# First expert stage of a fused transformer block: half of its first 64 tiles multiply both activation parts at once, in 512 columns, and VectorE adds the halves

## What is computed

```
q  = (xc @ w_q).reshape(t, PEER_HEADS, 2, PEER_QDIM // 2)
sc = einsum('thpc,hpnc->thpn', q, sub_keys)
v_half, i_half = lax.top_k(sc, 16)            # per half key
cand = v_half[:, :, 0, :, None] + v_half[:, :, 1, None, :]
top_s, pos = lax.top_k(cand.reshape(t, heads, -1), 16)
g = softmax(top_s)                             # weights of the 16 picks
act = gelu(einsum('thkd,td->thk', u_tab[expert], xc))
w = g * act
out = einsum('thk,thkd->td', w, v_tab[expert])
```

## Time and profile before

| | us |
|---|---|
| median of three runs | 2315.11 (2314.62 to 2317.86) |
| the profiled execution, its own time | 2312.29 |
| its span in the trace | 2310.5 |
| TensorE busy | 2226.4 (96%) |
| VectorE busy | 1700.3 (74%) |
| ScalarE busy | 1169.5 (51%) |
| mean granted clock of TensorE | 0.986 |

### The profile page before, as it was taken

How to read it: one execution, slowest core, us unless ns; L and a number is a source line. 1 busy time by engine, 2 the same in 40 slices (tenths; PEclk the granted TensorE clock), 3 DMA queues, 4 the chain that set the end, 5 groups by cost and what they waited for, 6 DMA issues and landing times.

```text
span 2310.5 us, 44458 instructions
## 1 busy us (share of the span) xinstructions
PE 2226.4 (96%) x15960; PEld 2011.1 (87%) x15960; DVE 1700.3 (74%) x3205; ACT 1169.5 (51%) x1688; POOL 0.2 (0%) x4
## 2 busy tenths in 40 slices
PE   7999899899999999999999998999999999999998
PEld 7998787689999999878888887899999998888886
DVE  5787676855998687798755567569977778986554
ACT  5566344545555555444444455545564554444444
POOL 0000000000000000000000000000000000000000
PEclk9999999799999999999999999999999999999999
DMA  6444244234545444455555542435554444555553
GB/s 262 178 180 152 92 149 149 73 107 149 177 169 190 156 168 168 146 172 173 183 190 190 191 153 79 155 137 173 181 179 158 172 165 149 178 166 190 190 190 137
DMA packets 95589, 376.37 MB, mean 163 GB/s; under 512 B 10861, under 2 KB 10989, under 8 KB 92817
## 3 DMA queue, kind: packets, MB, share of 16 engines
q1 hardware_dynamic: 95504, 375.29, 47.0%
HBM read 374.20 MB, written 1.05 MB: 162 GB/s over the span
## 4 chain that ended last, share of the span: by engine, by line
PE 70%; DVE 16%; ACT 2%; issue 2%; DMA 0%; ACTq 0%; SPq 0%; DVEq 0%
PE bank L328 21%; PE bank L330 21%; PE bank L329 21%; DVE tile_lo L2269 4%; PE bank L2003 3%; DVE e_hidden L2295 2%; DVE e_hidden L2289 2%; DVE e_hidden L2301 1%; DVE e_hidden L2341 1%; DVE e_hidden L2343 1%; DVE e_hidden L2339 1%; PE bank L2087 1%; DVE tile_lo L260 0%; PE bank L295 0%; PE bank L875 0%
## 5 line engine op out<-in xcount | busy, mean ns | idle before, releaser
L329 PE MATMUL bank<-a_lo,tile_hi 128*128 128x256 f32 x2688 | 756.1, 281 | 0.0
L328 PE MATMUL bank<-a_hi,tile_hi 128*128 128x256 f32 x2176 | 623.1, 286 | 16.4 <-DVE tile_lo L2269 5.3
L330 PE MATMUL bank<-a_hi,tile_lo 128*128 128x256 f32 x2176 | 613.7, 282 | 0.0
L329 PEld LDWEIGHTS bank<-a_lo,tile_hi 128*128 128x128 f32 x2688 | 511.4, 190 | 0.0
L2221 ACT ACTIVATE tile_hi<-wbuf 128x1024 fp32r<-128x1024 f32 x248 | 263.4, 1062 | 388.3 <-PE bank L330 385.4
L328 PEld LDWEIGHTS bank<-a_hi,tile_hi 128*128 128x128 f32 x2176 | 413.1, 190 | 24.1 <-issue 13.7
L2393 DVE TENSOR_TENSOR tile_lo<-wbuf,tile_hi 128x1024 fp32r<-128x1024 f32 x256 | 312.3, 1220 | 164.2 <-ACT tile_hi L2221 164.2
L330 PEld LDWEIGHTS bank<-a_hi,tile_lo 128*128 128x128 f32 x2176 | 413.3, 190 | 0.0
L328 PE MATMUL bank<-tile_hi,hidden_hi 128*128 128x512 f32 x1024 | 407.4, 398 | 5.0 <-DVE hidden_lo L2396 5.0
L330 PE MATMUL bank<-tile_hi,hidden_lo 128*128 128x512 f32 x1024 | 402.7, 393 | 0.0
L329 PE MATMUL bank<-tile_lo,hidden_hi 128*128 128x512 f32 x1024 | 402.4, 393 | 0.0
(11 more groups left out here) (355 smaller groups left out, 3112.6 us busy)
## 6 DMA issues: line engine op xcount, KB each, us to landing
wbuf<-in_peer_u SPq DMA_DIRECT2D x256, 512.0 KB, 3.5
wbuf<-in_peer_v SPq DMA_DIRECT2D x256, 512.0 KB, 3.5
wbuf<-in_w_in SPq DMA_DIRECT2D x16, 2048.0 KB, 7.7
wbuf<-in_peer_q SPq DMA_DIRECT2D x32, 512.0 KB, 4.0
wbuf<-in_hyb_in SPq DMA_DIRECT2D x16, 512.0 KB, 3.6
wbuf<-in_mla_uq SPq DMA_DIRECT2D x9, 512.0 KB, 3.5
wbuf<-in_mla_in SPq DMA_DIRECT2D x8, 528.0 KB, 3.3
wbuf<-in_w_v SPq DMA_DIRECT2D x2, 2048.0 KB, 7.2
```

Of the source, the lines that this page charges most:

```text
L328: nc.tensor.matmul(out, hi[:, cols], other_hi, start=start, stop=False, **kw)
L329: nc.tensor.matmul(out, hi[:, cols], other_lo, start=False, stop=False, **kw)
L330: return nc.tensor.matmul(out, lo[:, cols], other_hi, start=False, stop=stop, **kw)
```

## The change

In both expert layers, for tiles 0 to 63 (`SPLIT` = 8 rounds), every second pair of tiles (the pairs that begin at a tile number divisible by four) is multiplied in another way. For each step `k` there are two matmuls instead of three: the weight low part by the activation high part, 256 columns, into the right half of a bank; and the weight high part by both activation parts at once, 512 columns, into the whole bank. So the left half collects high by low and the right half the other two. Each tile of such a pair has a bank of its own, 2 and 3. The other pairs keep the three products and all use bank 1.

The two halves have to be added. ScalarE copies the left halves of both banks into `hidden` (128x512), VectorE adds the right halves to them in place (128x512), and ScalarE puts the sum through Gelu in place. TensorE may begin the next such pair once VectorE has added the one before (`parts_added`). VectorE's add of the pair `a - 1, a` stands in its list behind the low part of tile `a + 4`. The semaphores of the first layer that are now cleared for reuse add eight clears to SyncE's list behind the loads of the first U.

```
+def paired_products(nc, out, main, hi, lo, parts, other_hi, k, start, stop):
+    cols = slice(k * P, (k + 1) * P)
+    nc.tensor.matmul(out[:, main * S:(main + 1) * S], lo[:, cols], other_hi, start=start, stop=False, skip_group_check=True)
+    return nc.tensor.matmul(out, hi[:, cols], parts, start=False, stop=stop, skip_group_check=True)
...
+        def split_experts(r, j):
+            q, slot = j // 2, (M_U + j) % SLOTS
+            pe.wait_ge(lo_done, STEP * r + j + M_U + 1)
+            if j % 4 == 0:
+                pe.wait_ge(parts_added, 2 * r + q // 2 + 1)
+            if j % 4 == 2:
+                pe.wait_ge(bank_free, 2 * r + q // 2 + 2)
+            for k in range(KT):
+                if q % 2 == 0:
+                    last = paired_products(nc, bank[:, 2 + j % 2, :], 1, tile_hi[:, slot, :], tile_lo[:, slot, :],
+                                           g["a_parts"][:, :, k, :], h_hi[:, k, :], k, k == 0, k == KT - 1)
+                else:
+                    last = three_products(nc, bank[:, 1, (j % 2) * S:(j % 2 + 1) * S], tile_hi[:, slot, :], tile_lo[:, slot, :],
+                                          h_hi[:, k, :], h_lo[:, k, :], k, k == 0, k == KT - 1)
...
-        with pe.Fori(0, FIRST_WEIGHING) as r:
+        with pe.Fori(0, SPLIT) as r:
             for j in range(STEP):
-                experts(r, j)
+                split_experts(r, j)
+        pe.wait_ge(parts_added, 1 + ADDED)
+        for j in range(STEP):
+            experts(SPLIT, j)
...
+        def split_tile(r, j):
+            q = j // 2
+            if j % 4 == 1:
+                act.wait_ge(used, STEP * r + 2 * q + M_U + 2)
+                nc.scalar.activation(pair(r, q), split_banks(slice(0, S)), ACT.Copy).then_inc(low_kept, 1)
+            elif j % 4 == 3:
+                act.wait_ge(parts_added, 2 * r + q // 2 + 2)
+                gelu(r, q)
+            else:
+                act.wait_ge(used, STEP * r + j + M_U + 1)
+            rounded_u(r, j)
+            if j % 4 == 3:
+                nc.scalar.activation(pair(r, q - 1), pair(r, q - 1), ACT.Gelu).then_inc(added_done, 1)
...
+        def add_parts(a):
+            if a % SLOTS == 1 and a < SPLIT * STEP:
+                part = hidden[:, a - 1:a + 1, :]
+                dve.wait_ge(low_kept, a // SLOTS + 1)
+                nc.vector.tensor_tensor(part, split_banks(slice(S, 2 * S)), part, ALU.add).then_inc(parts_added, 1)
+
         def next_rest():
             nonlocal tiles
             if tiles < (FIRST_WEIGHING - 1) * STEP:
                 rest(tiles, tiles % SLOTS)
+                add_parts(tiles - SLOTS)
                 tiles += 1
```

More of the change, by code:

```diff
@@ L131, in build @@
         _, h_at = fixed("h_T", [P, KT, S])
-        _, other_at = fixed("h_other", [P, KT, S])
+        fixed("h_other", [P, KT, S])
         wbuf, wbuf_at = fixed("wbuf", [P, NW, SLOTS * TILE])
@@ L159, in build @@
             "tile_lo": rounded("tile_lo", [P, SLOTS, TILE], wbuf_at + 2 * BUF),
-            "a_hi": rounded("a_hi", [P, KT, S], other_at),
-            "a_lo": rounded("a_lo", [P, KT, S], h_at),
+            "a_parts": rounded("a_parts", [P, 2, KT, S], h_at),
             "hidden_hi": rounded("hidden_hi", [P, SLOTS, S], x_at),
@@ L170, in build @@
         }
+        g["a_lo"], g["a_hi"] = (g["a_parts"][:, part, :, :] for part in range(2))
         early = []
@@ L408, in first_layer @@
         conv_step, pool_step, conv_sig, gate_sig, z_sig, gated, v_done, v_kept = (
-            sem(n) for n in ("conv_step", "pool_step", "conv_sig", "gate_sig", "z_sig", "gated", "v_done", "v_kept"))
+            g["early_sem"](n) for n in ("conv_step", "pool_step", "conv_sig", "gate_sig", "z_sig", "gated", "v_done", "v_kept"))
         sig_flat = sig[:, :, :].rearrange("p a t -> p (a t)")
@@ L1932, in expert_layer @@
     sc_kept = [sem(f"{tag}_sc_kept{n}") for n in range(2)]
-    bank_free = sem(f"{tag}_bank_free")
+    bank_free, low_kept, parts_added, added_done = (sem(f"{tag}_{n}") for n in ("bank_free", "low_kept", "parts_added", "added_done"))
     half_step, best_step, pick_step, soft_step, exps_done, picks_turned, picks_kept = (
@@ L2022, in expert_layer, with split_banks @@
     FIRST_WEIGHING = ROUNDS - WEIGHING
+    SPLIT = FIRST_WEIGHING - 1
+    ADDED, OTHERS = 2 * SPLIT, 2 + 2 * SPLIT
+    def split_banks(cols):
+        return bank[:, 2:4, cols]
     at = 0
@@ L2099, in experts @@
             if j % 2 == 0:
-                pe.wait_ge(bank_free, STEP // 2 * r + j // 2 + 1)
+                pe.wait_ge(bank_free, STEP // 2 * r + j // 2 + OTHERS - 1 - STEP // 2 * SPLIT)
             for k in range(KT):
@@ L2103, in experts @@
                                       h_hi[:, k, :], h_lo[:, k, :], k, k == 0, k == KT - 1)
+            last.then_inc(used, 1)
+        def split_experts(r, j):
[12 more added lines that the diff above has]
+                                          h_hi[:, k, :], h_lo[:, k, :], k, k == 0, k == KT - 1)
             last.then_inc(used, 1)
@@ L2177, in scalar @@
         act.sem_inc(bank_free, 2)
+        act.sem_inc(parts_added, 1)
         def rounded_u(r, j):
@@ L2196, in tile, with pair @@
             rounded_u(r, j)
+        def pair(r, q):
+            return hidden[:, bass.ds(STEP * r + 2 * q, 2), :]
+        def split_tile(r, j):
[11 more added lines that the diff above has]
+                nc.scalar.activation(pair(r, q - 1), pair(r, q - 1), ACT.Gelu).then_inc(added_done, 1)
         def rounds(first, end):
@@ L2201, in rounds @@
                     tile(r, j)
-        rounds(0, FIRST_WEIGHING - 1)
+        with act.Fori(0, SPLIT) as r:
+            for j in range(STEP):
+                split_tile(r, j)
         act.wait_ge(soft_step, NT)
@@ L2350, in vector @@
             rest(a, a % SLOTS)
+            add_parts(a - SLOTS)
         for t in range(NT):
@@ L2371, in vector @@
         dve.wait_ge(picks_kept, 5)
-        dve.wait_ge(bank_free, 2 + HALF // 2)
+        dve.wait_ge(bank_free, OTHERS + HALF // 2 - 2 * ADDED)
+        dve.wait_ge(added_done, ADDED)
         one_hots(dve, 0, 0, 0, first_done[0], hots_done[0])
```

## The result

| | before | changed |
|---|---|---|
| median, us | 2314.86 (2310.33 to 2317.86, 4 runs) | 2334.62 (2333.33 to 2337.53, 4 runs) |
| ratio | | 1.0097, 95% interval 1.0084 to 1.0110 |
| profiled execution, its span | 2312.29, 2310.5 | 2337.53, 2335.7 |
| first stage, layer 1 and layer 2 | 211.67, 211.69 | 224.64, 223.29 |

The changed kernel is slower by 0.97%. The predicted time was 2336.1 us, in a range from 2330 to 2342.

The account below looks back on a forecast made before the run. VectorE's list was taken to bound tiles 5 to 57, TensorE's the rest. Each layer: 11.2 - 0.51 - 0.16 = 10.5 us; both layers 21.0, so 2315.1 + 21.0 = 2336.1 us, range 2330 to 2342.

Parts of the forecast that it names:

- The bound: First stage: VectorE's list sets the time for tiles 5 to 57 (3.05 us a tile against 2.86), TensorE's behind them.
- The adds: VectorE's list: 16 adds of 128x512 a layer, 0.60 us each, 13 of them ahead of tile 57's low part.
- The table load: ScalarE's 1.28 us load moves to the second pair, removing VectorE's idle time at tile 5: 0.6 us gained.
- The new wait: TensorE's tile 56 needs the add of pair 52, 53, behind tile 57's low part; it starts at 741.1, 11.2 us later.
- The wide matmuls: TensorE's paired tiles: a step goes from 0.357 to 0.352 us, saving 0.04 us a tile, 0.16 for four.
- The sum without the clock: First stage, each layer: 11.2 us later at tile 56, less 0.51 and 0.16, gives 10.5 us.
- the handover: At tile 56: TensorE waits for one more tile of VectorE's list plus the add before the path becomes TensorE's.
- The step that failed: TensorE's 3.6 us waits ahead of tiles 28 and 56: halved clock given chance 0.12, total 2339 to 2343 us.
- The rival: Half clock behind tile 56's wait loses 1.5 to 3 us a layer; tile 28's loss is taken up; chance 0.12.
- What was to show it: Profile signs: VectorE without gaps, one TensorE wait per four tiles up to 3.6 us, tile 56 near 741, clock 1.00.

Follow-up runs that it names:

- 24 spare matmuls: Changed kernel plus 24 extra 256-column matmuls ahead of TensorE's waits at tiles 28 and 56 in each layer: 2337.45 us, ratio 1.0099.
- the respaced one: Changed kernel with a low part after every 5 cells instead of 8 in the two selections over 128 values: 2325.44 us, ratio 1.0050.

## Why the prediction was right, and where it was off

**The number.** 2336.1 us against 2334.62 is closer than the account behind it. In the profiled execution the stages grew by 24.6 us and the span by 25.2, where 21.0 was forecast; that the median grew by only 19.8 is scatter between runs, and part of the closeness is luck, since a second set of runs of the same kernel stands 24.4 over the kernel before. The parts below are therefore judged by the stages.

**The bound.** Right. VectorE's list bounds tiles 5 to 57: sixteen adds alone, thirteen of them ahead of the low part of tile 57, bring 7.8 us a layer, taking them away brings back all of it, and spreading the same selection over six tiles more takes 5.6 us off the kernel before.

**The adds.** 0.60 us a step was taken from the earlier trace rows, and 0.60 was measured (742.00 to 742.60). The Trainium skill's rule, by which the next operation waits until the pipeline is empty ("VectorE: DVE Perf Modes", Terms), would have made it 0.68, taken as the end of the record; the trace doesn't agree.

**The table load.** The 0.54 us of idle time ahead of the low part of tile 5 are gone: it starts at 574.65, 8.25 us behind tile 0, and before it was 573.56 - 564.60 = 8.96. That is 0.71, and 0.6 was taken.

**The new wait.** The low part of tile 57 was to begin at 739.2 and tile 56 at 741.1, on the clock on which tile 0 begins at 564.60. Tile 0 is at 566.40 now, 1.80 later, so the rows above give 739.05 and 740.94.

**The wide matmuls.** 0.04 us a tile was taken. From tile 56 to the transposes, without a fall (24 spare matmuls), it is 786.77 - 741.10 = 45.67 us; before it was 776.27 - 729.90 = 46.37, less the 0.51 of the wait for tile 57, 45.86. So four paired tiles save 0.19, and 0.16 was expected.

**The sum without the clock.** 10.5 us a layer predicted, 222.00 - 211.67 = 10.3 measured. Its parts: the run without adds gives back 0.9 (210.80; 0.6 + 0.16 in the prediction), the adds in the list bring 7.8 on top of that, 218.6, and the handover is what is left up to 222.0, 3.4 us (in the prediction 11.2 - 7.2 - 0.51 = 3.5). That the three simply add up is taken here, not shown by a run of its own; the run with the adds sooner, 2.85 less where 2.8 was expected, bears the handover out.

**The step that failed.** The chance of 0.12 for a fall of the clock. I knew two rows, 2.16 us of idle time without a fall and one idle time with a fall, which is 5.05 us long in the trace, and put 3.6 us between them with little weight on the fall, though it lies midway. And the trace of the kernel before held two more falls, which the prediction doesn't use: one behind 2.50 us and one behind 1.69 us of idle time. Three rows of its timeline, two of them with the window behind them (the granted clock is the third number from the end):

```profile
349.86 1.97 PE L295 MATMUL bank<-cst,x_tok 128*128 128x128 f32 x8 [5.05 <-DVE x_tok L1044]
...
960.48 0.50 PE L328 MATMUL bank<-tile_hi,hidden_hi 128*128 128x512 f32 x1 [2.50 <-DVE hidden_lo L2396]
962.00:965.00 3.00, 3.00 (x16) 2.09 (x15) 3.00 (x7) 0.14 (x1) 0.00 (x0) 0.50 0.47 175
...
1337.62 0.63 PE L328 MATMUL bank<-tile_hi,a_hi 128*128 128x352 f32 x1 [1.69 <-DVE a_lo L308]
1337.00:1340.00 3.00, 2.38 (x8) 2.41 (x9) 0.76 (x2) 0.21 (x1) 0.00 (x0) 0.57 0.10 34
```

The same wait of 2.50 us in the second expert layer (before 1929.15) left the clock at 1.00. So the length of the idle time alone doesn't decide, as the prediction had it ("somewhere between 2.2 and 5 us"), and a fall was to be reckoned with at 3.6 us. It fell in all twelve waits of 3.27 us and over that the profiles show (four in each execution of the changed kernel, four in the respaced one). The rival's mechanism and place were right: what falls ahead of tile 28 is taken up, what falls ahead of tile 56 is not. Its size, 1.5 to 3 us a layer, is about what came: 1.3 in three stages, 2.6 in one. So the likeliest case was the forecast with this rival's loss in it: 2 x (10.3 + 1.3), 23 us, and not 21. The medians can't tell the two: their difference was 19.8 us the first time and 24.4 the second.

**What was to show it.** All but one came as written: VectorE without gaps, low parts 53 and 57 about 15 us apart (14.96), waits up to 3.6 us (3.50), steps of 0.233 us for the wide matmul (749.12 to 749.36 is 0.24), TensorE's busy time hardly changed, layers alike within 2 us (1.35). The exception is the clock, 1.00 only outside the two long waits.

## What to carry to other kernels

Where two engines are both full, find out which list the other ends up waiting for before lightening either: here eight matmuls a tile were taken from the engine that wasn't the bound, worth 0.05 us a tile since one of 512 columns costs nearly as much as two of 256, and paid with 0.15 us a tile on the one that was. When a release moves onto another instruction of a list, count what stands ahead of it there: one low part and one large operation more cost 3.4 us a layer, nearly half of what the adds themselves cost. And before adding work to a list or taking it away, try spreading it: the same list in another spacing was worth 9.6 us.

## What the runs showed of the hardware

- The clock fell behind every idle time of TensorE from 3.27 to 3.50 us (12 of 12), behind none from 0.9 to 1.85 us in the changed kernel's stages, but behind 1.84 us in one case, where twelve spare matmuls stood ahead of it, and behind the 1.80 us of the wait for the picks in 10 of 22 cases. This last wait is nearly the same in each of them (1.79 to 1.90 us, and 1.80 both with a fall and without), with the same six transposes ahead of it, so neither its length nor what ran just before it tells whether the clock falls. What does was not settled.
- The fall doesn't always show in the first matmul (0.38 us at 1632.47, then 0.61), and behind the wait for the picks it began 0.4 to 1.6 us after the matmuls had started again. Behind the long waits it lasted for 9 to 11 matmuls, about 3 us, and in two stages for 17 or 18, 5.5 us.
- A kernel whose own clock falls are few still spreads by 8 us from run to run (2330.4 to 2338.6), with the mean granted clock from 0.987 down to 0.982. A term of 1 or 2 us is better read from a stage of the profile than from the medians.
